# A hybrid transformer forward pass with 64 experts: ninth weight buffer loaded before the mixers end, last load cut into row groups, and the end computed row tile by row tile

## What is computed

```
h = rmsnorm(x, ffn_norm_w)
group, then top-2 experts of 8 in that group      # router: 8 groups x 8 experts
for each of 64 experts e (its tokens only):
    y_e = (silu(h @ w1[e]) * (h @ w3[e])) @ w2[e]  # w1, w3: 1024x512; w2: 512x1024
x = x + sum_e weight_e * y_e
out = rmsnorm(x, final_norm_w)                     # over 1024 columns of each token
```

## Time and profile before

| | before |
|---|---|
| median of 3 runs | 1614.3 us (1611.4 to 1615.96) |
| profiled execution, device time | 1613.9 us |
| its span, first to last instruction | 1612.0 us |
| TensorE busy / VectorE / ScalarE | 91% / 38% / 31% |
| expert weights read | 192 x 2 MB |
| issue to landing of a 2 MB expert load, median | 41.0 us |

### The profile page before, as it was taken

How to read it: one execution, slowest core, us unless ns; L and a number is a source line. 1 busy time by engine, 2 the same in 40 slices (tenths; PEclk the granted TensorE clock), 3 DMA queues, 4 the chain that set the end, 5 groups by cost and what they waited for, 6 DMA issues and landing times.

```text
span 1612.0 us, 22419 instructions
## 1 busy us (share of the span) xinstructions
PE 1469.1 (91%) x9481; PEld 895.4 (56%) x9481; DVE 620.3 (38%) x1368; ACT 501.4 (31%) x1086; POOL 0.2 (0%) x4
## 2 busy tenths in 40 slices
PE   8999999989999999899999988888888889988886
PEld 7777877878776788644444433433333434433332
DVE  5777666666654657621222211111111211211112
ACT  6666666666545655301111110011011001100102
POOL 0000000000000000000000000000000000000000
PEclk9999999999999999999999999999999999999999
DMA  7422442343232257899999999999999999999995
GB/s 275 163 105 104 145 156 105 131 144 138 90 126 105 105 209 284 327 428 427 428 427 427 427 428 427 426 427 427 428 428 427 428 427 427 426 427 428 427 428 208
DMA packets 72682, 496.53 MB, mean 308 GB/s; under 512 B 6240, under 2 KB 10624, under 8 KB 47616
## 3 DMA queue, kind: packets, MB, share of 16 engines
q1 hardware_dynamic: 72576, 495.03, 75.2%
HBM read 493.96 MB, written 1.05 MB: 307 GB/s over the span
## 4 chain that ended last, share of the span: by engine, by line
DMA 43%; PE 42%; DVE 8%; ACT 5%; issue 1%; SPq 0%; DVEq 0%; ACTq 0%
DMA arena<-in_expert_w 42%; PE ps L1127 16%; PE ps L1473 5%; PE ps L1480 4%; DVE arena L2018 3%; PE ps L1124 2%; PE ps L1494 2%; DVE w_lo L2018 2%; PE ps L1505 2%; ACT w_hi L1612 2%; ACT arena L1609 2%; ACT arena L1612 1%; PE ps L1223 1%; PE ps L1455 1%; DMA arena<-in_w_mem_kv 1%
## 5 line engine op out<-in xcount | busy, mean ns | idle before, releaser
L1473 PE MATMUL ps<-arena 128*32 128x512 f32 x2048 | 249.2, 605 | 90.3 <-DMA arena<-in_expert_w 90.2
L2015 DVE COPY arena<-ps 128x512 f32<-128x512 f32 (+2 forms) x203 | 114.9, 589 | 509.9 <-PE ps L1473 410.5
L1612 ACT ACTIVATE arena<-ps 128x512 f32<-128x512 f32 (+5 forms) x244 | 121.5, 500 | 544.2 <-PE ps L1494 292.3
L2018 DVE TENSOR_TENSOR w_lo<-arena,w_hi 128x512 fp32r<-128x512 f32 (+2 forms) x304 | 200.7, 673 | 146.9 <-ACT w_hi L1612 146.3
L1480 PE MATMUL ps<-arena 128*128 128x512 f32 x512 | 256.9, 625 | 0.0
L1612 ACT ACTIVATE w_hi<-arena 128x512 fp32r<-128x512 f32 (+2 forms) x320 | 193.5, 620 | 78.0 <-PE ps L1127 67.3
L1473 PEld LDWEIGHTS ps<-arena 128*32 128x32 f32 x2048 | 55.8, 109 | 234.0 <-DMA arena<-in_expert_w 143.1
L1127 PE MATMUL ps<-w_hi,hT_hi 128*128 128x512 f32 (+3 forms) x448 | 177.5, 396 | 4.4 <-ACT arena L1609 1.5
L1505 PEld LDWEIGHTS ps<-arena 128*128 128x128 f32 x1024 | 130.9, 194 | 86.6 <-issue 84.6
L1127 PE MATMUL ps<-w_hi,hT_lo 128*128 128x512 f32 (+3 forms) x448 | 168.3, 376 | 0.0
L1127 PE MATMUL ps<-w_lo,hT_hi 128*128 128x512 f32 (+3 forms) x448 | 167.6, 374 | 0.0
(11 more groups left out here) (154 smaller groups left out, 1372.3 us busy)
## 6 DMA issues: line engine op xcount, KB each, us to landing
arena<-in_expert_w SPq DMA_DIRECT2D x191, 2048.0 KB, 41.0
arena<-in_w_in SPq DMA_DIRECT2D x24, 2048.0 KB, 7.8
arena<-in_w_out SPq DMA_DIRECT2D x6, 2048.0 KB, 7.9
arena<-in_w_mem_kv SPq DMA_DIRECT2D x2, 2048.0 KB, 12.2
arena<-in_w_branch_hgrn SPq DMA_DIRECT2D x2, 2048.0 KB, 8.1
arena<-in_w_branch_mla SPq DMA_DIRECT2D x2, 2048.0 KB, 7.8
arena<-in_w_in SPq DMA_DIRECT2D x2, 1536.0 KB, 6.5
arena<-in_mla_w_uq SPq DMA_DIRECT2D x2, 1152.0 KB, 5.6
```

Source lines behind the costliest of these rows:

```text
L1473: o = e.matmul(B[32 * j:32 * j + 32, :], Xs[:, k, q:q + 32], Wn[:, k, :], start=i == 0, stop=i == 1)
L1612: return e.activation(o, i, ACTF.Copy, scale=scale)
L2015: return e.tensor_copy(o, i)
L2018: return e.tensor_tensor(o, a, b, op)
```

## The change

`RING` gets slot 8 as its second entry, and all later loads move one place. Loads 0 and 1 go at the end of the gates, and 2 to 8 wait for what 1 to 7 waited for (load 2 for the use of projection piece `NU - 3`). So that slot 8 is free, `ghi` and `glo` are cut into halves that live elsewhere (168, 172, 180 and 120 KB); the second half of `glo` has one more wait on VectorE, for `("logits", 0)`, because it lies on memory that TensorE's first router matmuls read.

The last load becomes sixteen DMAs of 8 rows (partitions), each row 16 KB. The residual goes into the four banks by four TensorE matmuls with the identity, one behind each of experts 9 to 12. Expert 63 gets an order of its own on TensorE. The end runs by token tile.

```diff
-        ghi, glo = rounded("g_hi", 184, 2, 1024), rounded("g_lo", 192, 2, 1024)
+        ghi = rounded("g_hi0", 168, 2, 512), rounded("g_hi1", 180, 2, 512)
+        glo = rounded("g_lo0", 172, 2, 512), rounded("g_lo1", 120, 2, 512)
...
-        RING = [7, 1 - NU % 2, 4, NU % 2, 6, 2, 3, 5, 8]
+        RING = [7, 8, 1 - NU % 2, 4, NU % 2, 6, 2, 3, 5]
...
+            def residual(t, h):
+                e.matmul(acc[t][h][:, :], ident, xk[:, t, :].rearrange("p (k c) -> p c k", k=8)[:, 64 * h:64 * h + 64, :],
+                         start=False, stop=False)
...
+            def combine_last():
+                ex = NE - 1
+                w.wait_ge(*at("ct", ex))
+                for t in range(2):
+                    for h in range(2):
+                        w.wait_ge(*at("ys", ex, h))
+                        e.matmul(acc[t][h][:, :], CT[ex % 2][:, t * 128:t * 128 + 128], Ys[:, h * 512:h * 512 + 512],
+                                 start=False, stop=True).then_inc(mark(pe_moe, ("sum", t, h)), 1)
...
-                w.wait_ge(*((s_last[h], 16) if ex == NE - 1 else expert_landed(m)))
+                w.wait_ge(*((s_last, 256) if ex == NE - 1 else expert_landed(m)))
...
+                if 9 <= ex < 13:
+                    residual(*divmod(ex - 9, 2))
...
+            end_squares(0, 0)
+            end_squares(0, 1)
+            end_squares(1, 0)
+            end_root(0)
+            end_squares(1, 1)
+            end_root(1)
...
+                if half:
+                    w.wait_ge(*at("logits", 0))
...
+            weigh(0)
+            end_mean(0)
+            weigh(1)
+            end_rsqrt(0)
+            end_mean(1)
+            end_out(0)
+            end_rsqrt(1)
+            end_out(1)
...
-                elif m == 8:
-                    w.wait_ge(*at("in x", 0, 7))
...
-                    for h in range(2):
-                        cs = slice(h * 512, h * 512 + 512)
-                        e.dma_start(expert_slot(m)[:, :, cs], src[:, :, cs]).then_inc(s_last[h], 16)
+                    for q in range(4):
+                        for r in range(4):
+                            rows = slice(32 * q + r, 32 * q + 32, 4)
+                            e.dma_start(expert_slot(m)[rows], src[rows]).then_inc(s_last, 16)
...
+            for t, h in ((0, 1), (0, 0), (1, 0), (1, 1)):
```

More of the change, by code:

```diff
@@ L1456, in gather @@
                     else:
-                        e.matmul(B, ghi[:, t, ks], hot, start=t == 0, stop=False)
-                        i = e.matmul(B, glo[:, t, ks], hot, start=False, stop=t == 1)
+                        part = slice(k % 4 * 128, k % 4 * 128 + 128)
+                        e.matmul(B, ghi[k // 4][:, t, part], hot, start=t == 0, stop=False)
+                        i = e.matmul(B, glo[k // 4][:, t, part], hot, start=False, stop=t == 1)
                 i.then_inc(mark(pe_x, ("in x", g, k)), 1)
@@ L1523, in tensor @@
                 gather(0, n, k)
-            for ex in range(NE):
+            for ex in range(NE - 1):
                 g = ex // 8
@@ L1552, in tensor @@
                     turn_c(ex)
[L1553 to L1554 removed]
+                if 9 <= ex < 13:
+                    residual(*divmod(ex - 9, 2))
+            ex = NE - 1
+            up(ex, 0)
+            combine(ex - 1, 0)
+            turn_h(ex, 0)
+            combine(ex - 1, 1)
+            turn_c(ex)
+            up(ex, 1)
+            turn_h(ex, 1)
+            down(ex, 0)
+            down(ex, 1)
+            combine_last()
             w.wait_ge(*at("flag"))
@@ L1851, in scalar @@
                     w.wait_ge(*at("new x", 2, half, t))
-                    copy(ghi[:, t, cs], xk[:, t, cs]).then_inc(mark(act_moe, ("ghi", half, t)), 1)
+                    copy(ghi[half][:, t, :], xk[:, t, cs]).then_inc(mark(act_moe, ("ghi", half, t)), 1)
                 elif kind == "mean x":
@@ L2666, in vector @@
[L2666 to L2673, removed]
@@ L2674, in vector, with end_mean @@
-            weigh(1)
[L2675 to L2678, removed]
+                w.wait_ge(*at("end squares", t, 0))
+                tt(weighed[:, t, :], acc[t][0][:, :], fw[:, 0:512], ALU.mult).then_inc(mark(dve_norm, ("weighed", t)), 1)
+            def end_mean(t):
+                ms = guess["late"][0][:, t:t + 1]
+                w.wait_ge(*at("end squares", t, 0))
+                ts(ms, ends[:, t:t + 1], 1.0 / D, EPS, ALU.mult, ALU.add).then_inc(mark(dve_norm), 1)
+                w.wait_ge(*book.newest)
+                w.wait_ge(*at("end squares", t, 1))
+                stt(ms, ends[:, 2 + t:3 + t], 1.0 / D, ms, ALU.mult, ALU.add).then_inc(mark(dve_norm, ("ms", "end", t)), 1)
@@ L2682, in vector @@
             with e.If(over > 0):
-                w.wait_ge(*at("out", 1, 0))
+                for t in range(2):
+                    for h in range(2):
+                        copy(x[:, t, h * 512:h * 512 + 512], acc[t][h][:, :]).then_inc(fv_x, 1)
                 for i, B in enumerate((*acc[1], B4, B5)):
```

84 lines of the change are left out of this document (46 added, 38 removed).

## The result

| | before | after |
|---|---|---|
| median of 7 runs each, same chip | 1615.12 us (1611.4 to 1615.96) | 1619.55 us (1616.72 to 1623.24) |
| ratio, 95% interval | | 1.0026 (1.0017 to 1.0036) |
| profiled execution, device time | 1613.9 us | 1616.72 us |
| its span | 1612.0 us | 1614.9 us |

A forecast was written before the change was run, and what follows sets the result against it. Expert loads were taken to set the pace from about 860 on, one per 4.9 us. From 1613.9, savings of 1.5 (early ninth load) and 3.0 (end), all else 0, gave 1609.4 us; range 1606.8 to 1613.2.

The forecast's parts named there:

- Part 1: Start of the expert load stream: issuing the ninth load early makes later loads land sooner, saving 1.5 us (0 to 3.0).
- the first rival: Lead of the early ninth load kept whole, no half clock in expert 1, good end: 1607.7 us; chance 0.12.
- Part 2: Residual on TensorE in experts 9 to 12: four matmuls, 3.7 us (7.4 at half speed), hidden behind loads: 0.
- Part 3: New order of expert 63: `down` starts at 1595.7 instead of 1595.54, counted as 0 (-0.2 to +0.5).
- Part 5: End by token tile: span ends 13.5 us after `down` starts instead of 16.5, 3.0 us saved (2.0 to 3.6).
- Part 4: Last load (w2 of expert 63) as sixteen DMAs of 8 rows: 0 us lost, 3.5 kept as the other bound.
- Engines behind: Last load runs on the eight DMA engines that are behind: 3.5 us lost, 1612.9 us; chance 0.18.
- writes in each other's way: Eight engines ahead take the last load; shared-row writes slow both, w3 late: 1611.2 us, possibly 1612.5; chance 0.19.

## Why the prediction was wrong, by its steps

**Part 1** held in its mechanism, and its 1.5 is met as a mean of two cases only, which is luck. The tenth load lands 7.6 after its issue, at an empty queue. By the medians the ninth load alone measured 0.9993 of 1615 us, -1.1 (-2.6 to +0.3), and together with the other parts 0.9977 against 0.9986, -1.5, with intervals that overlap. The profiles tell more. The table counts from the issue of the tenth load to the issue of load 14 and to the start of the last w1 product, in the kernels whose w1 isn't held up by the last load:

| | granted clock, 706 to 708 | issue of load 14 | w1 product of expert 63 |
|---|---|---|---|
| before | 0.50 | 27.5 | 900.8 |
| before, sixteen DMAs alone | 1.00 | 24.2 | 900.8 |
| ninth load early alone | 0.50 | 27.5 | 900.7 |
| changed, last load whole | 0.50 | 27.5 | 900.9 |
| changed, two column halves | 1.00 | 24.2 | 897.8 |
| changed | 1.00 | 24.2 | 898.0 |

Two lines of it, the first with the ninth load early alone and the second with two column halves:

```profile
706.00:708.00 2.00, 2.00 (x6) 0.97 (x4) 0.00 (x0) 0.00 (x0) 0.00 (x0) 0.50 0.93 393
...
706.00:708.00 2.00, 2.00 (x16) 0.83 (x19) 0.73 (x2) 0.07 (x1) 0.00 (x0) 1.00 0.97 410
```

So the early ninth load wins 3.0 us where TensorE runs expert 1 at full clock, and nothing where it falls to half clock; in neither case 1.5. The first is the condition of the first rival, and the profiled execution of the changed kernel ran so. At half clock load 14 does land 1.5 earlier, as forecast (35.2 after the issue of the tenth load, for 36.7). But load 16 (issued at 719.79 and 13.0 under way, before at 717.29 and 13.2), counted in the same way, lands at 46.4 for 46.6, and the lead is gone. The DMA engines had stood nearly idle ahead of load 14 (share 0.20 and 0.08 in 712 to 714), where at full clock, in the changed kernel, their share stays at 0.84 or more from 708 to 713. I take it that this idle time is what the lead is lost to; the landing of load 14 by itself doesn't show all of it. How many executions run at which clock isn't known: of the thirteen profiles with an early ninth load four had the full clock.

**Part 2** held in its result. TensorE waits for nothing between 800 and 870. Its duration was taken too short: with the strided operand the two records of one matmul take 1.98 us, at a granted clock of 1.00, against 0.92 in the earlier trace rows, so 7.9 and not 3.7 in all. That is near the text's other value, 7.4, and it is hidden as well.

```profile
811.19 1.98 PE L1488 MATMUL ps<-arena 128*128 128x512 f32 x2
```

**Part 3** held: `down` starts 11.0 after the w1 product where no load is late, for 10.9.

**Part 5** held: 13.2 from `down` to the end of the span, for 13.5. Parts 3 and 5 together give -3.1 in the spans (24.2 against 27.3) and -2.3 (-3.7 to -1.0) by the medians, for a forecast of -3.0.

Without part 4 the sum, 4.5 us or 0.9972, would have stood by the medians: the three kernels with another last load measured 0.9977, 0.9977 and 0.9972.

**Part 4** is the step that failed: "I take 0, nearest to the rows of the stream". It measured 7.3 us in the profiled executions of the changed kernel and of the one with two halves: 5.2 of a later `down`, 1.7 of half clock and some 0.4 in the stores. By the medians it is 8.0. There were three faults in it.

First, the value. The part itself had a bound for eight engines behind, 3.5, and the runs show 3.0 for that alone; it was set aside for the row that was nearest, though that row was of a DMA of another shape. Of the engines the packets tell something. The pages of three kernels, with the last load as sixteen DMAs of 8 rows, as one of 128 rows and as eight of 128 rows:

```profile
DMA packets 71883, 496.53 MB, mean 307 GB/s; under 512 B 6337, under 2 KB 10721, under 8 KB 46689
...
DMA packets 71771, 496.53 MB, mean 308 GB/s; under 512 B 6225, under 2 KB 10609, under 8 KB 46577
...
DMA packets 72778, 496.53 MB, mean 308 GB/s; under 512 B 6336, under 2 KB 10720, under 8 KB 47712
```

Seven more DMAs of 128 rows bring 111 more packets under 512 B, or about 16 each. Sixteen DMAs of 8 rows in place of one of 128 bring 112 more, so they have 128 together, or 8 each. The Trainium skill (DMA: Bandwidth & Descriptors, section "Why a DMA increments its semaphore by 16 and not by 1") gives eight engines for 8 rows, with a last write to the semaphore from each; these counts agree. In what followed from it, the eight were taken to be all ahead or all behind. The share of 0.12 at 49 GB/s at the end, about two engines' worth, says that they were mixed, and two that are behind are enough: `down` waits until they are done.

Second, the rivals were kept apart. "Engines behind" (+3.5) and "writes in each other's way" (+1.8 to +3.1) were weighed as two cases, and each had its chance. Both came at once, 3.0 and 2.2, and the range, up to 1613.2, reached little beyond the larger of them. The second was played down with "no row shows two engines slowing each other", which was true of the trace and no evidence: no expert load in it has another shape than 128 rows. The Trainium skill (SBUF — State Buffer, section "Door 1: The DMA port swizzle") has rows 64 to 127 on ports of their own. The four kernels that write one half twice agree: the loads in front are slowed where rows 64 to 127 are written and not where rows 0 to 63 are, whatever is read. By the same section of the Trainium skill 16 rows side by side reach four ports, and by its formula every eighth row reaches eight, from which I expected the time of the last load to double again; 1.0023 and 1.0026 don't show that.

Third, a cost had no place in the sum at all. In the wait of 5.45 us for a load TensorE stood idle, and the clock was at its lower level under the very work on which the end hangs. A late load was priced by its lateness alone.

What stays open: why 16 rows in either pattern run at half rate and no less, and with it whether the harm comes from two engines that write through one port or from something else that goes with the rows. That the place written decides is shown; that the port is the reason is not. Why some engines are so far ahead of others at the end of a stream of equal loads, the share falling from 1585 on with the last landing near 1594.7 before, wasn't tested either.

## To carry to other kernels

Cut a large load by columns, so that each piece keeps all 128 rows: two, eight or one piece cost the same, while pieces of 8 or 16 rows cost 7 to 12 us more here, and slow the loads in front of them too. Where a change gives a transfer a shape that the trace doesn't show, its bounds from the nearest rows must be able to add up, and the range has to hold their sum. A load that ends up as late as here, 5 us, on a path that TensorE waits on is to be priced with the work behind it at half clock. And a lead at the start of a stream of loads has to be followed until the queue stays full: here it was 3.0 us, and all of it was gone where the queue ran dry once more.

The best kernel here is the change with its last load whole or in column pieces, 0.9972 to 0.9977 of the kernel before, some 4 us faster.

## What the runs showed of the hardware

- Sixteen DMAs of 8 rows (128 KB each) and eight of 16 rows both leave the DMA engines at a share near 1.0 with 213 to 246 GB/s in the windows shown, about half of the 427 of 128-row loads, while other loads are in flight. Eight DMAs of 128 rows don't.
- A DMA of 128 rows leaves about 16 packets under 512 B, one of 8 rows leaves 8.
- A DMA slows loads that were issued before it, on the same queue: w3 of expert 63 took 50.2 us from issue to landing with rows 64 to 127 written twice, 41.9 with rows 0 to 63, and the place written in SBUF decided it.
- In a wait of 5.45 us TensorE's granted clock fell to 0.50, and with 18 matmul records in it the clock stayed at 1.00.
- The early ninth load won 3.0 us with the granted clock of expert 1 at 1.00 and nothing at 0.50, where the DMA share fell to 0.08 ahead of load 14.
- A matmul of 128x512 fp32 whose moving operand is strided took 1.98 us instead of 0.92.
